# First expert chunk in a place of its own, sample products of the gather on two row tiles, and an earlier load of the final norm's weight

## What is computed

```python
logits = xt @ w_router + b_router            # 264 x 32 experts
top_v, top_i = lax.top_k(logits, 4)
gates = softmax(top_v)
# for every expert e and the tokens that chose it:
gu = xb @ w_gate_up[e] + b_gate_up[e]        # 1024 x 2048 weights
gate, up = minimum(gu[:, :1024], 7), clip(gu[:, 1024:], -7, 7)
act = (up + 1) * (gate * sigmoid(1.702 * gate))
y[tokens of e] += (act @ w_down[e] + b_down[e]) * gates   # 1024 x 1024 weights
# then x + y, and a final rmsnorm with the weight norm_final
```

## Time and profile before

| | us |
|---|---|
| median of 3 runs | 1423.47 |
| lowest and highest | 1421.4, 1425.28 |
| profiled execution | 1423.71 |
| its span, first to last instruction | 1421.9 |

### The profile page before, as it was taken

How to read it: one execution, slowest core, us unless ns; L and a number is a source line. 1 busy time by engine, 2 the same in 40 slices (tenths; PEclk the granted TensorE clock), 3 DMA queues, 4 the chain that set the end, 5 groups by cost and what they waited for, 6 DMA issues and landing times.

```text
span 1421.9 us, 16452 instructions
## 1 busy us (share of the span) xinstructions
PE 1390.5 (98%) x6532; PEld 740.1 (52%) x6532; DVE 412.5 (29%) x1076; ACT 254.5 (18%) x561; POOL 35.7 (3%) x56
## 2 busy tenths in 40 slices
PE   9999999999999999999999999999999999999897
PEld 8888878887888543343333433333334333343233
DVE  3754465785321221121111211212112111121112
ACT  2013364484201210110101101001010010110002
POOL 1000012110000000000000000000000000000000
PEclk9999999999999899999999999999999999999999
DMA  9444547896876489999999999999999999999994
GB/s 242 135 147 138 167 143 235 277 354 212 288 229 262 147 342 414 428 427 428 428 426 427 429 427 429 426 427 427 428 427 427 428 427 429 427 428 427 428 425 186
DMA packets 105329, 488.63 MB, mean 344 GB/s; under 512 B 10051, under 2 KB 73755, under 8 KB 78583
## 3 DMA queue, kind: packets, MB, share of 16 engines
q1 hardware_dynamic: 96616, 460.47, 80.7%
q0 software_dynamic: 4608, 24.41, 4.8%
q10 hardware_dynamic: 4034, 2.72, 0.7%
HBM read 476.64 MB, written 11.19 MB: 343 GB/s over the span
## 4 chain that ended last, share of the span: by engine, by line
PE 81%; DMA 12%; ACT 3%; DVE 2%; issue 1%; ACTq 0%; POOL 0%; SPq 0%; POOLq 0%; DVEq 0%
PE bank L295 79%; DMA ring<-in_w_down 5%; DMA plain_conv<-in_w_down 5%; DMA ring<-in_w_gate_up 2%; PE bank L891 2%; ACT ring L684 1%; DVE ring L1515 0%; DMA small<-y_dram 0%; DVE plain_conv L1512 0%; ACT plain_conv L609 0%; ACT ring L640 0%; DVE exn L1515 0%; ACT ring L635 0%; ACT ring L644 0%; ACT ring L633 0%
## 5 line engine op out<-in xcount | busy, mean ns | idle before, releaser
L295 PE MATMUL bank<-ring,plain_conv 128*64 128x512 f32 x2304 | 518.3, 598 | 4.7 <-DMA ring<-in_w_down 4.0
L295 PEld LDWEIGHTS bank<-ring,plain_conv 128*64 128x64 f32 x2304 | 158.2, 137 | 322.7 <-issue 320.5
L295 PE MATMUL bank<-plain_conv 128*64 128x512 f32 (+5 forms) x1072 | 269.3, 525 | 4.9 <-issue 4.3
L295 PE MATMUL bank<-exn,ring 128*128 128x264 f32 (+1 forms) x1168 | 265.6, 389 | 2.8 <-ACT plain_conv L581 2.6
L295 PEld LDWEIGHTS bank<-exn,ring 128*128 128x128 f32 (+1 forms) x1168 | 220.4, 190 | 44.5 <-issue 5.0
L1729 DVE TENSOR_TENSOR xT<-xT,bank 128x264 f32<-128x264 f32 x128 | 54.9, 429 | 489.7 <-PE bank L295 488.7
L295 PEld LDWEIGHTS bank<-plain_conv 128*64 128x64 f32 (+3 forms) x1072 | 116.0, 160 | 101.0 <-issue 95.2
L295 PE MATMUL bank<-exn,plain_conv 128*64 128x512 f32 x384 | 114.7, 596 | 1.8 <-DMA plain_conv<-in_w_down 1.8
L787 ACT ACTIVATE plain_conv<-plain_conv 128x512 f32<-128x512 f32 x32 | 20.1, 629 | 378.6 <-DVE plain_conv L1734 378.6
L1734 DVE TENSOR_SCALAR plain_conv<-bank 128x512 f32<-128x512 f32 x32 | 22.0, 688 | 209.7 <-PE bank L295 209.7
L295 PE MATMUL bank<-ring 128*128 128x264 f32 (+3 forms) x520 | 80.4, 336 | 0.0
(11 more groups left out here) (273 smaller groups left out, 656.5 us busy)
## 6 DMA issues: line engine op xcount, KB each, us to landing
ring<-in_w_gate_up SPq DMA_DIRECT2D x96, 2048.0 KB, 24.0
ring<-in_w_down SPq DMA_DIRECT2D x48, 2048.0 KB, 26.6
ring<-in_w_in SPq DMA_DIRECT2D x36, 1024.0 KB, 5.3
exn<-in_w_gate_up SPq DMA_DIRECT2D x15, 2048.0 KB, 25.6
plain_conv<-in_w_gate_up SPq DMA_DIRECT2D x15, 2048.0 KB, 27.0
exn<-in_w_down SPq DMA_DIRECT2D x7, 2048.0 KB, 25.5
plain_conv<-in_w_down SPq DMA_DIRECT2D x7, 2048.0 KB, 25.7
ring<-in_w_proj_b SPq DMA_DIRECT2D x8, 1024.0 KB, 6.6
```

The costliest lines, as they stand in the source:

```text
L295: return nc.tensor.matmul(out, w, x, start=start, stop=stop)
```

## The change

1. Chunk 0 of a pass gets a ninth place, `lead` (4096 columns of `plain_conv` from 512 on, that is under the activations' and the hidden values' buffers, which are first written when the chunk has been used). It is loaded behind load number 6 of `w_proj_b`. Chunks 1 to 8 then fill the eight places, and chunk n goes into place (n - 1) mod 8. The rule of waits in `load_pair` stays. Buffers move to make room: `y_out`, `w_router`, the gathered tokens' halves, and the junk outputs of the squares.
2. The load of `n_final` moves from behind chunk 11's to behind that of `lead`.
3. The 8 sample rows of `u_tok` and of `slot_of` are repeated over all partitions in pair 0 (`repeat_samples`: a product with the new 0/1 matrix `repeat`, written by DVE ahead of `row_of`; DVE copies the slots out, ACT the tokens). The gather of each pair then does the sample products of two column groups c and c + 2 one behind the other, one with rows 0 to 7, one with rows 32 to 39, into two banks, and the large products after them.
4. A few semaphores are merged (`x_var` into `ssq0_set`, `columns_set` and `rows_set` into `spread_set`).

```diff
+        repeat = sb("repeat", [TS, P])
-        y_out = plain_t[:, 3584:4608]
+        y_out = plain_t[:, 4608:5632]
+        lead = plain_t[:, 512:512 + WIDE]
...
+            def load_lead(j):
+                sp.dma_start(lead, chunk_rows(j, 0)).then_inc(S["lead_landed"], 16)
...
-                        for chunk in (2, 3):
-                            load_chunk(0, chunk, chunk)
+                        for slot in (2, 3):
+                            load_chunk(0, slot + 1, slot)
                         load_half(7, 1)
                         load_half(6, 0)
+                    if k == 2 * KT and c == 6:
+                        load_lead(0)
+                        sp.dma_start(n_final, a["norm_final"].rearrange("(o d) -> o d", o=1).to_broadcast([P, D])).then_inc(S["final_loaded"], 16)
...
                     sp.wait_ge(S["w_used"], CHUNKS * i + (c + 1 - MSLOT))
...
-                        load_chunk(j, c, (CHUNKS * r + c) % MSLOT)
+                        load_chunk(j, c, (CHUNKS * r + c - 1) % MSLOT)
...
-            load_pair(0, 0, 0, first=MSLOT)
-            sp.dma_start(n_final, a["norm_final"].rearrange("(o d) -> o d", o=1).to_broadcast([P, D])).then_inc(S["final_loaded"], 16)
+            load_pair(0, 0, 0, first=MSLOT + 1)
...
+                    with act.If(p < 1):
+                        act.wait_ge(S["rep_filled"], 2)
+                        for h in range(2):
+                            nc.scalar.copy(u_tok[:, 2, 512 * h:512 * h + 512], p_y[h][:, :]).then_inc(S["rep_taken"], 1)
...
+            def gather_samples(c0):
+
+                for c in (c0, c0 + 2):
+                    gather_part(p_xt[c % 4 // 2][:, QUAD * (c % 2):QUAD * (c % 2) + QUAD], c, 2, True, False, 32 * (c % 4 // 2))
+
+            def gather_prompt(c):
+
+                for t in range(2):
+                    ins = gather_part(p_xt[c % 4 // 2][:, QUAD * (c % 2):QUAD * (c % 2) + QUAD], c, t, False, t == 1)
+                if c % 2:
+                    ins.then_inc(S["xt_filled"], 1)
+
+            def repeat_samples():
+
+                mm(p_ht[:, 0:E], repeat[:, :], slot_of[0:TS, 2, 0:E], True, True).then_inc(S["rep_filled"], 1)
+                for h in range(2):
+                    ins = mm(p_y[h][:, :], repeat[:, :], u_tok[0:TS, 2, 512 * h:512 * h + 512], True, True)
+                ins.then_inc(S["rep_filled"], 1)
...
                             ins.then_inc(S["pg_filled"], 1)
+                            repeat_samples()
                     if kk == (2 if first else 0):
...
+                        if first:
+                            pe.wait_ge(S["slots_taken"], 1)
...
                     pe.wait_ge(S["pick_ready"], g + 1)
-                    for c in range(3):
-                        gather(p_xt[c // 2], 4 * r + c)
+                    if first:
+                        pe.wait_ge(S["rep_taken"], 2)
+                    gather_samples(4 * r)
+                    gather_prompt(4 * r)
+                    gather_prompt(4 * r + 2)
+                    gather_samples(4 * r + 1)
+                    gather_prompt(4 * r + 1)
                     pe.wait_ge(S["ht_ready"], 2 * i + 1)
                     turn_hidden(2 * i + 1)
-                    gather(p_xt[1], 4 * r + 3)
+                    gather_prompt(4 * r + 3)
...
+            V.tensor_copy(repeat.rearrange("p (r q) -> p r q", q=TS), ident[0:TS, 0:TS].unsqueeze(1).to_broadcast([TS, P // TS, TS]))
+            done("spread_set", V.tensor_copy(row_of, ident[0:GROUPS, 0:GROUPS].unsqueeze(2).to_broadcast([GROUPS, GROUPS, P])))
...
+            dve.wait_ge(S["rep_filled"], 1)
+            done("slots_taken", V.tensor_copy(slot_of[:, 2, 0:E], p_ht[:, 0:E]))
```

More of the change, by code:

```diff
@@ L274, in build @@
         p_u = [[ps[2], ps[6]], [ps[3], ps[7]], [ps[4], ps[0]]]
-        u_junk = [[plain_t[:, o:o + 512] for o in pair] for pair in ((512, 1536), (1024, 2048), (2560, 4608))]
+        u_junk = [[u_tok[:, t, 512 * h:512 * h + 512] for h in range(2)] for t in range(3)]
         p_logits, p_rank0, p_rank12, p_total = ps[5], ps[1], ps[2], ps[1]
@@ L341, in _, with chunk_rows, load_chunk, load_half @@
             w_gu, w_dn = a["w_gate_up"][0], a["w_down"][0]
-            def load_chunk(j, c, slot):
+            def chunk_rows(j, c):
                 if c < KT:
                     k = c % 4
[L347 to L356, removed]
+                    return w_gu[2 * j + c // 4, 2 * P * k:2 * P * k + 2 * P, :].rearrange("(p s) n -> p (s n)", s=2)
+                k = (c - KT) // 2
+                return w_dn[2 * j + c % 2, 4 * P * k:4 * P * k + 4 * P, :].rearrange("(p s) n -> p (s n)", s=4)
+            def load_chunk(j, c, slot):
+                sp.dma_start(wide[slot], chunk_rows(j, c)).then_inc(w_landed[slot], 16)
+            def load_lead(j):
+                sp.dma_start(lead, chunk_rows(j, 0)).then_inc(S["lead_landed"], 16)
+            def load_half(slot, s):
+                w = slice(SLOT * s, SLOT * s + SLOT)
+                sp.dma_start(wide[slot][:, w], chunk_rows(0, slot + 1)[:, w]).then_inc(w_landed[slot], 16)
             for w, k in ((a["w_proj_a"], KT), (a["w_proj_b"], 2 * KT), (a["w_out"], KT)):
@@ L393, in load_down_half, with load_pair @@
                              src).then_inc(S[f"half{x}_landed"] if h else w_landed[slot], 16)
-            def load_pair(i, r, j, first=0, final=False):
+            def load_pair(i, r, j, first=0, final=False, leads=False):
                 for c in range(first, CHUNKS):
+                    if leads and c == 0:
+                        sp.wait_ge(S["w_used"], CHUNKS * i)
+                        load_lead(j)
+                        continue
                     sp.wait_ge(S["w_used"], CHUNKS * i + (c + 1 - MSLOT))
@@ L419, in _ @@
                 with sp.Fori(1, n_passes) as p:
-                    with sp.Fori(0, PAIRS // ROUND - 1) as q:
+                    for r in range(ROUND):
+                        load_pair(PAIRS * p + r, r, r, leads=r == 0)
+                    with sp.Fori(1, PAIRS // ROUND - 1) as q:
                         for r in range(ROUND):
@@ L1077, in _ @@
             project(9, KT, lambda k: plain[:, GATE + k, :], 0, 0, 5)
-            pe.wait_ge(S["columns_set"], 1)
+            pe.wait_ge(S["spread_set"], 1)
             b = open_bank("gn")
@@ L1152, in _, with gather_part @@
             u_cols = u_tok.rearrange("p t (k i s) -> p t k s i", i=P, s=2)
-            def gather_part(out, c, t):
-                return mm(out, u_cols[0:ROWS[t], t, c // 2, c % 2, :], pick[0:ROWS[t], t].rearrange("p w s -> p (w s)"), t == 0, t == 2)
+            def gather_part(out, c, t, start, stop, row=0):
+                rows = slice(row, row + TS) if t == 2 else slice(0, P)
+                return mm(out, u_cols[rows, t, c // 2, c % 2, :], pick[rows, t].rearrange("p w s -> p (w s)"), start, stop)
             def gather(out, c):
                 for t in range(3):
-                    ins = gather_part(out[:, QUAD * (c % 2):QUAD * (c % 2) + QUAD], c, t)
+                    ins = gather_part(out[:, QUAD * (c % 2):QUAD * (c % 2) + QUAD], c, t, t == 0, t == 2)
                 if c % 2:
                     ins.then_inc(S["xt_filled"], 1)
+            def gather_samples(c0):
[11 more added lines that the diff above has]
+                ins.then_inc(S["rep_filled"], 1)
             def first_part(c, t):
-                ins = gather_part(p_first[c // 2][c % 2][:, 0:QUAD], c, t)
+                ins = gather_part(p_first[c // 2][c % 2][:, 0:QUAD], c, t, t == 0, t == 2)
                 if t == 2 and c % 2:
@@ L1206, in pair @@
                 g = QUADS * p + quad
[L1208 to L1213, removed]
-                def arrived(c):
-                    slot, landed_by = chunk(c)
-                    pe.wait_ge(w_landed[slot], landed_by)
+                def arrived(c):
+                    if first and c == 0:
+                        pe.wait_ge(S["lead_landed"], 16 * p + 16)
+                        return lead
+                    n = CHUNKS * r + c - 1
+                    slot, rounds = n % MSLOT, ROUND * CHUNKS // MSLOT
+                    per_pass = rounds * QUADS - (1 if slot == MSLOT - 1 else 0)
+                    halves = 1 if slot >= 6 else 0
+                    pe.wait_ge(w_landed[slot], 16 * per_pass * p + 16 * rounds * quad + 16 * (n // MSLOT + 1 + halves))
                     return wide[slot]
@@ L1365, in _ @@
             link(V.memset(column_of, 0.0))
-            done("columns_set", V.memset(small[:, 712:728:GROUPS + 1], 1.0))
+            done("spread_set", V.memset(small[:, 712:728:GROUPS + 1], 1.0))
             dve.wait_ge(S["ssq0_set"], 1)
```

26 lines of the change are left out of this document (13 added, 13 removed).

## The result

The changed kernel takes 1425.78 us (median of 20 runs, 1420.69 to 1432.39), the kernel before 1423.39 us beside it (20 runs, 1418.01 to 1427.48). That is within the 0.3% that I had called the least to be told, and twenty runs of each do tell it from nothing. The forecast was 1424.5 us, 1.05 us slower.

What follows compares the result with a forecast made beforehand. Transfers run gapless once pair 0's `down(0)` ends (532.8 us), so only work ahead counts: 0.15 + 2.2 - 1.3 = +1.05 us, 1424.8 profiled, 1424.5 median; unknown prices give 1423.4 to 1427.1, the range 1418.0 to 1428.5.

Steps and rivals of the forecast that it cites:

- The frame: Whole kernel: end of pair 0's `down(0)` (532.8) + 851.8 us gapless transfers + 37.3 us tail + 1.8 us.
- The ninth place: Chunk 0's load taken out of the loop's time: costed at 0, since chunk 16 still waits for pair 0's `down(0)`.
- Its load and the norm's: Loads queued beside `w_proj_b`: 2.6 MB more take 6.1 us where 8 are free from 380 us; nobody waits.
- DVE's copy: Writing `repeat` ahead of `row_of`: 0.15 us taken, 0 to 0.46 possible, passed on in full by ACT's wait.
- The repeated samples: Three 8-row products on PE in pair 0, ahead of 532.8 us: 2.2 us more (1.6 to 2.6).
- The gather: Row tiles in pairs 0 to 13: 1.3 us saved a pair, ends 1.7 and -0.5; only pair 0's counts.
- all such waits: New waits behind pair 0's repeated samples, on DVE's slots and ACT's copies: all covered by over 2 us, 0.
- rival (d): Gather's row tiles run one after the other, only changes saved (0.75): 1.6 us in place of 1.05, 1425.0; chance 0.08.
- only pair 0's saving counts: Of 14 gather savings only pair 0's, ahead of `w_used` 9, counts; later ones only lengthen PE's wait for chunks.
- Rival (c): Each pair's gather: row tiles cost, binding from 1.9 us a pair; at 2.5, 12.7 us more, 1436; chance 0.07.
- Rival (e): Slow clock after 458 to 461 us moves: 1419.3 without it, 1427 to 1428 with a second half more; chance 0.10.

## Why the prediction was right, and where not

- **The frame** held: time of `down(0)` of pair 0, a fixed stretch, a fixed tail. The stretch is 852.4 us against 851.8 (851.9 to the landing of chunk 187), the tail 37.2 against 37.3. Adding 7.25 us ahead of the point gave +6.3 (3.6 to 9.0).
- **The ninth place at 0** held: 0.9994 (0.9982 to 1.0007) alone. Its load and the norm's fit beside `w_proj_b`: from 380 to 420 us the DMA share is 0.94 where the earlier trace rows have 0.80, and PE is busy for all of the 40 us, as before.
- **DVE's copy**, taken at 0.15 us: from the start of the copy to the first state step it is 0.53 us, against 0.46 for the one copy in the earlier trace rows, so 0.07.

```profile
288.06 0.34 DVE L1631 COPY repeat<-ident 8x128 f32<-8x128 f32 x1
288.19 0.47 DVE L1632 COPY ring<-ident 4x512 f32<-4x512 f32 x1
288.59 2.33 DVE L1559 SCALAR_TENSOR_TENSOR ring<-ring,rstd,exn 128x2048 f32<-128x2048 f32 x1
```

- **The repeated samples**, taken at 2.2 us: 2.73, a little above the dear end of 2.6. They run into the slower clock themselves, which began while they ran; at full clock, with 128 rows, they take 2.13.
- **The gather**, taken at 1.3 us saved: 6.70 less 5.2 is 1.5, and so is 57.28 less 55.75 for a pair. In pair 0 a wait of 0.26 us for ACT's copy takes a part of it back, because the work that covered this copy became shorter; the prediction had all such waits at 0. The 1.5 are near the 1.6 that the prediction had for samples side by side and twice the 0.75 for samples one after the other, so rival (d) is out. Nor does the time leave room for it: the 20 instructions with four samples' products take 4.19 us, and at 0.434 us a product six large ones need 2.6 and four small ones one after the other 1.7, which would be 4.3 without any change of shape. That only pair 0's saving counts was right: PE is busy 12.9 us less between 600 and 1300 us, and the transfers stand at 427 GB/s as before.
- **The step that was missing** is the clock behind the repeated samples. The prediction looked for waits behind these products and found them covered; it took the price of the products themselves from a line at full clock and asked nothing of the speed of what follows. The next chunk took 2.7 us more. With it, the sum is 0.1 + 2.7 + 2.7 - 1.5 + 0.3 = +4.3 us, where 3.4 (1.7 to 5.0) were measured. The direction and the range were right; of the size of the loss the forecast had a third. That the loss still fell between -0.1 and +3.6 us is luck: the range was that wide for the prices of the products, and none of it was meant for the clock.
- **Rival (c)**, more work on PE in each pair, had the right mechanism and a wrong point: it starts to bind at about 0.5 us a pair, not at 1.9 (6.5 us over 13 pairs). I had compared the rates and left the lead in hand out of the account. The changed kernel went the other way, so the forecast wasn't touched.
- **Rival (e)**, clock by chance: it is real, but as spread and not as a cause of the difference. Over the 14 profiled executions of all kernels the mean granted clock from 461 to 473 us lies between 0.57 and 1.00, mostly at 0.72.

## What to carry to other kernels

When both engines and transfers look full, find the last time at which the transfers stood idle and what ended it: only the work ahead of that point counts, and moving some of it behind the point pays until the next such wait takes over. Judge slack by the distance of two chains at their end, not by their rates. And products that use few rows can lower the clock for what follows: look at the granted clock behind them. Here filling their rows with zeros cost no time on PE.

## What the runs showed of the hardware that I had not expected

Three products of 8 rows, 2.5 to 3.1 us of PE time without an idle piece, brought the lower level of 1.2 GHz for 6.8 us in all three kernels that had them (mean granted clock from 489 to 497 us 0.57, 0.60 and 0.57); it began while the last of them ran. The same products with 128 rows did not, in both kernels that had those (1.00 and 1.00), nor did the place without them. PE counts as busy in the profile in either case.

Few rows don't always do this. The four products of 4 rows and 264 columns at 360.46, 1.97 us in all, leave the granted clock at 1.00 in both kernels (355 to 400 us). Where between the two the fall begins, and by what, no run shows.

A second such stretch sits in the mixer, behind a wait of PE of about 3 us for a trip through DRAM. It was there in the profiled execution of the changed kernel and absent in that of the kernel before, with the same work. Over 343 to 355 us, 7 of the 14 profiled executions have a mean clock of 0.86 or 0.87 and 7 have 1.00, kernels with and without the 8-row products in both groups. In the two lines the first is of the changed kernel:

```profile
343.00:346.00 3.00, 3.00 (x9) 2.28 (x8) 0.00 (x0) 0.00 (x0) 0.00 (x0) 0.50 0.15 35
```

```profile
343.00:346.00 3.00, 2.02 (x9) 1.79 (x10) 0.00 (x0) 1.10 (x4) 0.00 (x0) 1.00 1.00 287
```

The spread of the runs goes with the clock: of the 20 runs of the changed kernel, the two with a mean clock of 0.989 took 1420.7 and 1421.0 us, the two with 0.983 took 1431.9 and 1432.4. Which stretches were slow in them isn't known, since only one execution of each kernel was profiled.
